# Four slabs of query weights stay in four pair places through layer two's mixers, and the opening block of zero products grows from 8 to 15

## The reference, cut to what matters

```python
for l in range(2):
    h = rms_norm(x, norm1_g[l])
    proj = h @ w_in[l]                       # attention, convolution and recurrence
    x = x + mixed @ w_out[l]
    h2 = rms_norm(x, norm2_g[l])
    q = h2 @ peer_wq[l]                      # 1024 x 2048: the query weights
    # scores against two key tables, top 16 of each, top 16 of the 256 sums, for 8 heads
    hid = gelu(einsum("td,tkd->tk", h2, u_tab[experts]))    # 128 experts a token
    x = x + einsum("tk,tkd->td", gates * hid, v_tab[experts])
```

## Time and profile before

| | |
|---|---|
| median of 3 runs | 2016.06 us (2015.12 to 2018.51) |
| the profiled execution's own time | 2013.99 us |
| its span, first to last instruction | 2012.2 us |
| moved by DMA | 772.23 MB, 384 GB/s over the span |
| busy: PE, DVE, ACT, POOL | 87%, 64%, 43%, 29% |
| granted TensorE clock, mean | 0.978 |

### The profile page before, as it was taken

How to read it: one execution, slowest core, us unless ns; L and a number is a source line. 1 busy time by engine, 2 the same in 40 slices (tenths; PEclk the granted TensorE clock), 3 DMA queues, 4 the chain that set the end, 5 groups by cost and what they waited for, 6 DMA issues and landing times.

```text
span 2012.2 us, 21640 instructions
## 1 busy us (share of the span) xinstructions
PE 1755.8 (87%) x7082; PEld 993.5 (49%) x7082; DVE 1289.4 (64%) x3503; ACT 870.9 (43%) x2184; POOL 576.1 (29%) x517
## 2 busy tenths in 40 slices
PE   8999999999899989888779978977899898777776
PEld 4449865763578465464226535622464364222222
DVE  4224337677865367686776857688586677874444
ACT  2422214344488234723353573344437534443333
POOL 0000000023222233333343324344433344443331
PEclk9999999999999999989999988999999999999999
DMA  9769877499999999999999999999999999999996
GB/s 385 258 264 364 299 278 252 156 343 406 419 419 418 420 419 420 416 419 402 421 419 420 420 400 409 420 419 419 420 419 420 395 419 419 420 420 421 419 420 258
DMA packets 109105, 772.23 MB, mean 384 GB/s; under 512 B 12224, under 2 KB 12736, under 8 KB 17088
## 3 DMA queue, kind: packets, MB, share of 16 engines
q0 software_dynamic: 73728, 536.90, 64.7%
q1 hardware_dynamic: 35264, 233.95, 30.1%
HBM read 769.75 MB, written 1.05 MB: 383 GB/s over the span
## 4 chain that ended last, share of the span: by engine, by line
DMA 45%; PE 43%; DVE 5%; ACT 4%; issue 1%; POOL 0%; SPq 0%; DVEq 0%; POOLq 0%; ACTq 0%
DMA ring<-in_peer_dram,eidx 19%; PE psum L772 11%; PE psum L1189 11%; DMA arena<-in_peer_dram,eidx 11%; PE psum L795 7%; PE psum L1001 6%; DMA early<-in_peer_dram,eidx 5%; DMA kv<-in_peer_dram,eidx 5%; DMA ring<-in_slabs_dram 5%; PE psum L1018 2%; DVE ring L2118 1%; DVE arena L2118 1%; ACT diag L1534 1%; PE psum L870 1%; PE psum L972 1%
## 5 line engine op out<-in xcount | busy, mean ns | idle before, releaser
L2269 POOL DMA_INDIRECT arena<-in_peer_dram,eidx x206 | 229.8, 1116 | 843.8 <-DVE eidx L1990 428.7
L1189 PE MATMUL psum<-arena,diag 128*128 128x512 f32 x740 | 362.7, 616 | 78.0 <-ACT diag L1534 77.3
L1524 ACT ACTIVATE wexp<-wexp 128x1 f32<-128x1 f32 x512 | 103.3, 202 | 676.3 <-DVE wexp L2118 674.5
L2118 DVE CUSTOM_DVE_ANT_0 arena<-arena,osb 128x1024 f32<-128x1024 f32 x206 | 251.7, 1223 | 137.3 <-DMA arena<-in_peer_dram,eidx 134.6
L1189 PE MATMUL psum<-ring,diag 128*128 128x512 f32 x520 | 256.8, 619 | 42.9 <-ACT diag L1534 42.3
L1189 PEld LDWEIGHTS psum<-arena,diag 128*128 128x128 f32 x740 | 131.9, 192 | 270.0 <-ACT diag L1534 154.2
L2118 DVE CUSTOM_DVE_ANT_0 ring<-ring,osb 128x1024 f32<-128x1024 f32 x152 | 185.7, 1223 | 116.6 <-DMA ring<-in_peer_dram,eidx 115.6
L772 PE MATMUL psum<-ring,hT 128*128 128x512 f32 x528 | 243.0, 609 | 13.4 <-DMA ring<-in_slabs_dram 11.3
L2269 POOL DMA_INDIRECT ring<-in_peer_dram,eidx x152 | 172.6, 1136 | 257.4 <-PE psum L1189 196.5
L1189 PE MATMUL psum<-kv,diag 128*128 128x512 f32 x364 | 179.1, 615 | 42.7 <-ACT diag L1534 36.8
L1534 ACT ACTIVATE diag<-const,wexp 128x128 f32<-128x128 f32 x450 | 180.7, 402 | 16.6 <-PE psum L1189 1.9
(11 more groups left out here) (338 smaller groups left out, 2016.9 us busy)
## 6 DMA issues: line engine op xcount, KB each, us to landing
ring<-in_slabs_dram SPq DMA_DIRECT2D x199, 1024.0 KB, 5.8
ring<-in_slabs_dram SPq DMA_DIRECT2D x8, 768.0 KB, 4.3
kept<-in_slabs_dram SPq DMA_DIRECT2D x4, 1024.0 KB, 13.5
arena<-in_peer_dram,eidx POOLq DMA_INDIRECT x206
ring<-in_slabs_dram SPq DMA_DIRECT2D x6, 512.0 KB, 6.7
ring<-in_peer_dram,eidx POOLq DMA_INDIRECT x152
kk<-in_keys_dram SPq DMA_DIRECT2D x2, 1024.0 KB, 8.8
kv<-in_peer_dram,eidx POOLq DMA_INDIRECT x102
```

The source lines that it names most:

```text
L1189: ins = pe.matmul(bank(b), diags_of(n), pair(slot_of[n])[:, 1024 + 512 * h:1536 + 512 * h], start=(k == 0), stop=(k == 127))
L1524: act.activation(wn, wn, ACT.Gelu_apprx_tanh).then_inc(*up("gelu", n))
L2118: v.tensor_tensor_reduce(out=row, in0=row, in1=row_y[t], scale=1.0, scalar=0.0, op0=ALU.mult, op1=ALU.add, accum_out=wexp[:, c:c + 1]).the ...
L2269: pool.indirect_dma_start(pair(i), None, tables, bass.IndirectOffsetOnAxis(ap=eidx[:, 128 * t + k:128 * t + k + 1], axis=0)).then_inc(sig. ...
```

## The change

`LODGED` names two parts of the query weights, c = 1 and c = 2, and two places for each: (0, 1) and (4, 5). From gather 204 on (`LODGE`) these four places take no pair. In M10, ahead of its w_out slabs, SP waits until the last pair of before 204 in each has been used and loads the four slabs of layer two's query weights there (`lodge`). `feature_tile` reads c = 1 and c = 2 from there in M10 and in M11, and neither mixer loads them through the ring. A place takes pairs again once M11's products of its part are done, and POOL waits for that event at the first gather into it. The planner follows all of this, so the order of the work from there on is planned anew. START goes from 8 to 15. The constants of the planner stay.

```diff
--- before.py
+++ after.py
@@ -26,7 +26,9 @@
 NRING, NLATE = 6, 3
 LAG = 3
 
-START, NORM, MIX = 8, (0, 2), (0, 0, 3, 2, 4)
+LODGED, LODGE = {1: (0, 1), 2: (4, 5)}, 204
+
+START, NORM, MIX = 15, (0, 2), (0, 0, 3, 2, 4)
 ADD = ((0, 2), (6, 7), (0, 1), (6, 7))
 
 
@@ -437,6 +439,9 @@
         SLOT_FREE = (("o_turn", "M00"), ("wout", "M00", 1), ("wq", "M00", 3), ("key_scores", "M00", 3),
                      ("att_scores", "B1", 7), ("att_values", "B1", 7), ("att_counted", "B1", 5, 1))
 
+        def lodger(i):
+            return next((c for c in LODGED if i in LODGED[c]), None)
+
         tables = T["peer"]
 
         vector_pairs, on_tensor = set(), {}
@@ -476,7 +481,7 @@
             slots, pairs = dict(enumerate(SLOT_FREE)), {}
             landed, counts, tensor = {}, {"dot": 0, "weigh": 0}, []
             waiting = {"PE": [], "DVE": []}
-            left_of = {}
+            left_of, lodging = {}, set()
             for e in ENGINES:
                 for s in STAGES:
                     us = [sum(w[1] for w in way if w[0] == "run") for way in ways[e][s]]
@@ -664,7 +669,10 @@
                         load_slabs()
                     elif what == "emptied":
                         del landed[arg[0]]
-                        slots[pairs[arg[0]]] = ("accumulate" if on_vector(arg[0]) else "down_mm", arg[0])
+                        i = pairs[arg[0]]
+                        slots[i] = ("accumulate" if on_vector(arg[0]) else "down_mm", arg[0])
+                        if i in lodging and arg[0] < LODGE:
+                            slots[i] = ("wq", "M11", lodger(i))
                     way.pop(0)
                 going[e] = None
                 return True
@@ -681,6 +689,9 @@
                 for i in range(NRING - NLATE):
                     if n >= T_SHRINK and ("ring", i) not in seen and used.get(less[0] - NRING + i) in seen:
                         seen["ring", i] = seen[used[less[0] - NRING + i]]
+                if n == LODGE:
+                    lodging.update(i for i in slots if lodger(i) is not None)
+                    slots.update({i: ("wq", "M11", lodger(i)) for i in lodging if slots[i] != ("taken",) and slots[i] in seen})
                 free = [(seen[key], i) for i, key in slots.items() if key in seen]
                 if not free:
                     return False
@@ -779,11 +790,14 @@
                     if k % 2:
                         yield 1
 
-            def feature_tile(s, b, hT_, name, *key, resident=None):
+            def feature_tile(s, b, hT_, name, *key, resident=None, lodged=None):
 
                 for i in range(4):
                     if i % 2 == 0:
-                        if resident is None:
+                        if lodged is not None:
+                            weights = pair(LODGED[lodged][i // 2])
+                            w.wait_ge(sig.sem("l_lodged%d" % lodged), 32)
+                        elif resident is None:
                             weights, n = take(s)
                         else:
                             weights = kept[:, SLOT * (i // 2):SLOT * (i // 2) + SLOT]
@@ -794,12 +808,12 @@
                     for k in range(8):
                         ins = pe.matmul(bank(b)[:, 128 * i:128 * i + 128], wk[:, k, 128 * (i % 2):128 * (i % 2) + 128], hT_[:, k, :],
                                         start=(k == 0), stop=(k == 7))
-                    if i == 1 and resident is None:
+                    if i == 1 and resident is None and lodged is None:
                         ins.then_inc(*up("half", name, *key))
                         consumed[n] = ("half", name, *key)
                     if i == 3:
                         ins.then_inc(*up(name, *key))
-                        if resident is None:
+                        if resident is None and lodged is None:
                             consumed[n] = (name, *key)
                     yield 1
 
@@ -1136,7 +1150,8 @@
                 w.wait_ge(*at("turned_a", s, "x", 1))
                 for c in range(4):
                     b = b_[(1, 3)[c % 2]]
-                    for i, _ in enumerate(feature_tile(s, b, hTt, "wq", s, c, resident=l if c == 3 else None)):
+                    for i, _ in enumerate(feature_tile(s, b, hTt, "wq", s, c, resident=l if c == 3 else None,
+                                                         lodged=c if l == 1 and c in LODGED else None)):
                         yield 1
                         if i == 0 and c:
                             yield from key_scores(s, c - 1)
@@ -2257,7 +2272,9 @@
             pool.memset(diag[:, 0:128], 0.0).then_inc(sig.sem("blank"), 1)
             for n, i in gathers:
                 (l, t), k = ORDER[n // 128], n % 128
-                if i in held:
+                if i in held and held[i] < LODGE <= n and lodger(i) is not None:
+                    w.wait_ge(*at("wq", "M11", lodger(i)))
+                elif i in held:
                     w.wait_ge(*at("accumulate" if on_vector(held[i]) else "down_mm", held[i]))
                 elif i < 7:
                     w.wait_ge(*at(*SLOT_FREE[i]))
@@ -2370,12 +2387,24 @@
                     slab(S_GATE + c)
                     yield
 
+            def lodge():
+
+                for c in LODGED:
+                    for part, i in enumerate(LODGED[c]):
+                        n = max(n for n, j in gathers if j == i and n < LODGE)
+                        w.wait_ge(*at("accumulate" if on_vector(n) else "down_mm", n))
+                        sp.dma_start(pair(i), T["slabs"][S_MIX + 22 + 14 + 2 * c + part]).then_inc(sig.sem("l_lodged%d" % c), 16)
+
             def mixer(l, t):
                 if (l, t) == (0, 0):
                     for c in range(2, 4):
                         slab(S_QKV + c)
                         yield
                 for c in (3, 4, 0, 1, 2, 5, 6, 7, 8, 9):
+                    if (l, t, c) == (1, 0, 5):
+                        lodge()
+                    if l == 1 and c - 7 in LODGED:
+                        continue
                     for part in range(2):
                         if (l, t, c, part) == (1, 0, 3, 0):
                             small(1)
```

## The result

The changed kernel takes 2025.78 us (median of five runs, 2025.72 to 2027.99), the kernel before 2016.06 us (median of five, 2010.90 to 2018.51). The ratio is 1.0058, with a 95% interval of 1.0047 to 1.0069: slower by 0.58%, some 11.7 us (9.5 to 13.9; the two medians lie 9.7 us apart). The forecast was 2012.0 us, in a range to 2022. The profiled execution has a span of 2024.1 us against 2012.2.

A forecast was written before the change was run, and what follows sets the result against it. After 470 us the DMA channel, full at some 420 GB/s, was taken as the bound. Slabs -10.0, START -0.3, stalls +6.2, smooth running and SP's queue 0 gave -4.1 us: median 2012.0 us, range 2005 to 2022.

The forecast's parts named there:

- The bytes: M10 and M11 query weights: four loads of 1 MB less, wholly where the channel is full; -10.0 us.
- Six places in smooth running: From gather 204 to 1652 us: six places keep the channel full, 3.9 us to spare; cost 0, bounds 0 to 10.
- the two stalls: Once each in M10 and M11, the attention's last division on DVE waits for PE and no place comes free.
- 1.01 from 1306 to 1442 us: Sign that the forecast is right: the channel's share stays at 1.01 in this window, with gathers alone.
- Six places in a stall: Attention stalls with four gathers fewer queued: the channel idles 6.0 us in M10, 0.2 us in M11.
- The places come back late: Rival, 15%: in M11 POOL waits for the closed places and gathers behind wait too; 3.4 us, 2015.4 us, no change.
- SP's queue: SP's wait in `lodge` ahead of M10's w_out slabs is covered; cost 0, without that cover 11 us.
- START, -0.3 us: Start: seven more zero products give full clock, but the eleventh slab, some 3 us waited for, limits the gain to 0.3 us.
- Six places run dry: Rival, 20%: at both stalls the whole four transfers are missing; +9.7 us, 2025.8 us.

The follow-up runs named there:

- closed: Against the kernel before: four places closed from gather 204 until M11's query products, nothing loaded into them, all slabs through the ring, START 8; +13.7 us (1.0068).
- lodge8: The changed kernel with START 8 in place of 15, the lodging alone; +10.7 us against the kernel before (1.0053).
- closedboth: Against the kernel before: four places closed, four middle query-weight slabs of both M10 and M11 not loaded, the resident column standing in; +2.4 us (1.0012).

## Why the prediction was wrong

- **The bytes, -10.0 us.** Right by themselves (-10.5 and -8.5 with ten places). The second step that failed is "it lies wholly where the channel is full", and so that it can be added to the cost of six places. With six places the stretches in which slabs load run dry in part once the slabs are gone: eight slabs are worth 11.3 us there, and the lodging, which saves eight and loads four at a price of 8.3, gains 3.0 us (13.7 of `closed` less 10.7 of `lodge8`), not 10.
- **Six places in smooth running, 0.** Right where gathers run alone: 0.9 us idle in 200. But this 0 stood for all of gather 204 to 1652 us outside the two stalls, and there `closed` has some 7.7 us more idle than before, beside M10's stages above all. The forecast's own sign, 1.01 from 1306 to 1442 us, failed too: 0.99, at 407 GB/s, with the hole before 1340 us in it.
- **Six places in a stall, 6.0 + 0.2 us.** The step that failed first. All that closing the places costs is 13.7 us. By the windows the first stall itself lost 3.9 us more than before, under its price, and the second 6.3, where 0.2 stood. The work ahead at one gather was read as the whole reserve of each mixer, and a stall as a single event; but POOL stands still several times in a mixer. One more wait is seen in the changed kernel: ACT's for the routing's softmax (4.39 us, ahead of POOL's 7.58). What each adds was not measured by itself, and how much of the loss is the new order of the work and how much the places alone stays open.
- **The places come back late, 15%.** It did not happen: POOL waited 1.99 us for the query products.
- **SP's queue, 0.** Nothing that shows (`closedboth` and `lodge8`).
- **START, -0.3 us.** Right, in its mechanism too: the clock was 1.00 and the eleventh slab came at 45.96 us as before. The wait ahead of it is 0.98 us and not some 3, because PE waits 1.20 us for two slabs before. That the first slab's products begin at 8.20 in place of 8.50 us is owed to the slab: over the profiled executions of all these kernels they began between 7.15 and 9.21 us. The rule of the Trainium skill (TensorE: Matmul & The Clock Gate, "What's actually happening"), that activity releases the throttle, agrees: the clock did rise. The time didn't follow, since DMA sets it.
- **The rivals.** "Six places run dry" gave 2025.8 us, the measured time, at 20%. Its place and sign were right, its sum by luck: it had 19.96 us for the stalls and -10.3 for the rest, the runs have 13.7 for the places and -3.0 for the slabs. Its half sentence that the slabs that fill the second stall come later is nearest to what was found; the price of that, 7 us, stood in no term.
- **The range** ended at 2022 because one full stall was thought the worst likely; the two stalls were treated as separate chances, though the same lack of four places decides both.

## What to carry to other kernels

Where a channel looks full, ask what fills it at the moment each transfer runs: bytes saved in a stretch in which the other stream stands still are worth only what remains after they leave a hole (here 11.3 of 19.0 us for eight slabs). Take two edits that touch the same stretch as one, and price them in both states of the other. A reserve of buffers may cost nothing that shows at first and then much (here two places 1.2 us, three 3.8, four 13.7), so count all waits of a stage that follow each other, not the longest alone.

## What the runs showed of the hardware

The sixteen DMA engines do not stand level. In the kernel before, one works about 7 us longer than the rest after the last gather, though the page's slices show the channel full up to there. The last gather is issued at 1980.31 us and lands at 2000.67, when that engine is done, though the others have run dry by 1993; so part of the 20.38 us of the earlier trace rows is probably its queue and not the channel's. In `closed`, after long dry stretches, the tail is some 5 us shorter. What puts that engine behind was not looked for. The Trainium skill (Perfetto Trace Analysis, "What 'DMA-bound' means") lists specific DMA engines among the things that can bind a kernel; the tail agrees.
